# DeltaNet: the last inverse level as quarter-size products, and decay sums as two fp32r halves

## The chip, the cores and the metric

The kernel runs on one NeuronCore of a Trainium2 chip. The metric is device time in microseconds of one execution; the time before is 3436.42 us, the median of three runs (3434.37 to 3437.41). TensorE (PE) multiplies matrices, with its weight loads shown apart (PEld); VectorE (DVE), ScalarE (ACT) and GpSimd (POOL) work on tiles; SyncE (SP) issues most transfers.

## The reference, cut to what matters

The network has four layers, each a feed-forward block, a token mixer and a second feed-forward block. Layers 0 and 3 mix tokens with a bidirectional chunked gated DeltaNet of 8 heads of 128, on 128 context and 256 latent tokens; layer 1 is an attention layer, layer 2 a pooling mixer. The part that matters:

```
gcum = jnp.cumsum(cg(g), axis=-1)
diff = gcum[..., :, None] - gcum[..., None, :]
decay = jnp.where(incl, jnp.exp(jnp.where(incl, diff, 0.0)), 0.0)
lmat = jnp.where(strict, jnp.einsum('nbhid,nbhjd->nbhij', kb, k) * decay, 0.0)
amat = lmat + jnp.eye(CHUNK, dtype=F32)
sol = lax.linalg.triangular_solve(amat, rhs, left_side=True, lower=True, unit_diagonal=True)
attn = jnp.einsum('nbhid,nbhjd->nbhij', q, k) * decay
```

So there are exponentials of differences of running sums, and the solution of a unit triangular system for each chunk, head and direction. The kernel works on chunks of 128 tokens, which gives the same result.

## The kernel before, in words

Everything is written out by hand on each engine's queue; semaphores alone order the engines, and each queue runs in the order of the code.

A DeltaNet layer projects and convolves, then runs a *prelude*, a *decay stage* and three *waves*. There are 48 maps of 128 x 128 (3 chunks, 2 directions, 8 heads), handled four heads at a time in one PSUM bank of 512 columns, so twelve groups.

*Prelude* (`proj_a` on VectorE, start of `delta_net` on the others). TensorE forms the running sums; VectorE copies them to `dn_small` (L1425), forms their negative (`SM_NEG`, L1426) and the sum with the log of the gate (`SM_GB`, L1427) and signals `gcT_in`. TensorE, after the first two groups of key products, transposes the three 128 x 48 tables (L1968) and ScalarE copies them to `gcT` (L998), whose rows above 48 GpSimd has set to zero (L688).

*Decay stage.* For a group, `exponents` adds two things in a PSUM bank: a bf16 product that puts large negative numbers where the mask is off (L1953), and for each of four heads a product that spreads row `at` of `gcT` over all 128 partitions (L1957): the stationary operand is column `at` of the identity, broadcast to 128 columns. ScalarE takes the exponential with the other running sum as bias, four heads one by one (L1011), into a ring of three buffers (key half) or into `att` (query half). In the key half VectorE multiplies by the key products into `amap` (L1454), and GpSimd gathers the 16 x 16 diagonal blocks of the first eight groups (L702); for the last four VectorE copies them itself (L1452). The order is, six times: four key products, two decay groups; then six times: four query products, two decay groups, and ScalarE's copy of the query products (L1023). VectorE meanwhile inverts all diagonal blocks by forward substitution (L1466, L1467), transposes them (L1470, L1471) and spreads them into full tiles (L513), which needs the block mask that TensorE copies to PSUM after the whole stage (L1987). GpSimd spreads a second set (also L513).

*Waves.* A wave treats one chunk of each direction, in four groups `j`. It grows the inverse from blocks of 16 to 128 in three levels (4, 5, 6). For each level and group TensorE forms y = A'C (`y_product`, L2005), VectorE multiplies it with the level's mask into `W_Y` (L1500), TensorE forms z = B y (`z_product`, L2020) and VectorE subtracts it from the kept matrix (L1504). At levels 5 and 6 four transposes (`turn`, L2025) follow each y product, copied by ScalarE (L1040). At level 6, z updates C for the groups 0 and 1 and its transpose for 2 and 3. After it come the products with keys, values and state; value products of the first wave wait for GpSimd's `vb` (L726). After the last wave SP fetches the output weights, which lie in the same memory, once the last value products are done.

In the trace all products of four heads carry line L1932 (`four`). Each fp32 product of 128 x 128 is two TensorE instructions, so a group of four heads shows as x8; a transpose is one.

Of the kernel before, what the change touches and what calls it, by code (L numbers as in the profile page):

```python
# [46 lines left out]
LEVELS = (4, 5, 6)  # L47
WAVES = 3
# [83 lines left out]
def build(nc, inp, out, stages=3 * DEPTH):  # L132
# [143 lines left out]
    gcT = place("gcT", [P, 3, P], at=region_m + 11 * KB)  # L276
# [91 lines left out]
    gcT_zero, gcT_in, gcT_turned, gcT_copied = (sem(n) for n in ("gcT_zero", "gcT_in", "gcT_turned", "gcT_copied"))  # L368
# [259 lines left out]
    def _(pool):  # L628
# [50 lines left out]
        def delta_net(layer):  # L679
# [6 lines left out]
            pool.wait_ge(mask_in, 16 * (a + 1))  # L686
            pool.wait_ge(gc_done, a + 1)
            pool.memset(gcT[:], 0.0).then_inc(gcT_zero, 1)  # L688
# [108 lines left out]
    def _(act):  # L797
# [117 lines left out]
        def proj_a(ph):  # L915
# [81 lines left out]
            act.wait_ge(gcT_zero, a + 1)  # L997
            act.activation(gcT[0:MAPS], ps[5][0:MAPS, 0:T].rearrange("p (i c) -> p i c", i=3), ACT.Copy).then_inc(gcT_copied, 1)  # L998
# [188 lines left out]
    def _(dve):  # L1187
# [159 lines left out]
        def proj_a(ph):  # L1347
# [74 lines left out]
            steps.settle(dve.reciprocal(flat(SM_BETA), flat(SM_B)))  # L1422
            dve.wait_ge(gc_done, a + 1)
            both = dn_small[:, SM_GC:SM_TOTAL + 1].rearrange("p i c d h -> p (i c d h)")
            steps.settle(dve.tensor_copy(both, ps[4][:, 0:4 * NT * HEADS]))  # L1425
            dve.tensor_scalar(flat(SM_NEG), flat(SM_GC), -1.0, None, ALU.mult)  # L1426
            dve.tensor_tensor(flat(SM_GB), flat(SM_GC), flat(SM_NSP), ALU.add).then_inc(gcT_in, 1)  # L1427
# [3 lines left out]
        def delta_net(layer):  # L1431
# [3 lines left out]
            def bank(i):  # L1435
                return ps[i][:].rearrange("p (h c) -> p h c", h=GROUP)
# [56 lines left out]
            for w in range(WAVES):  # L1493
# [3 lines left out]
                for lev in LEVELS:  # L1497
                    for j in range(4):
                        mm(j, f"y{lev}")
                        dve.tensor_tensor(W_Y[j][:], bank(j), per_head(level_mask[lev - LEVELS[0]]), ALU.mult).then_inc(w_dve[j], 1)  # L1500
                    for j in range(4):
                        mm(j, f"z{lev}")
                        keep = (W_B if lev == LEVELS[-1] and j >= 2 else W_C)[w][j]
                        dve.tensor_tensor(keep, keep, bank(4 + j), ALU.subtract).then_inc(w_dve[j], 1)  # L1504
                    if w == 2 and lev == LEVELS[1]:
                        dve.wait_ge(c0_sq, a + 1)
                        dve.tensor_reduce(sumsq[:, 0:HEADS], first_sq, AX.X, ALU.add).then_inc(o_sum, 1)
# [228 lines left out]
    def _(pe):  # L1736
# [184 lines left out]
        def delta_net(layer):  # L1921
# [12 lines left out]

            def key_map(e):
                c, quad = MAP_ORDER[e]
                if e >= 2:
                    pe.wait_ge(amap_done, 2 * N_MAP * a + 2 * e - 2)
                keys = lambda h: k_of(c, GROUP * quad + h)
                four(e % 2, keys, keys).then_inc(kk_mm, 1)  # L1940
# [7 lines left out]
            def exponents(n, which, mask):  # L1948
# [6 lines left out]
                for h in range(GROUP):  # L1955
                    at = HEADS * (2 * c + d) + GROUP * quad + h
                    ins = pe.matmul(ps[bank][:, h * P:(h + 1) * P], ident[:, at:at + 1].to_broadcast([P, P]),  # L1957
                                    gcT[:, which], start=False, stop=h == GROUP - 1)
# [8 lines left out]
            for i, which in enumerate((SM_NEG, SM_GB, SM_GC)):  # L1967
                ins = pe.transpose(ps[5][0:MAPS, i * P:(i + 1) * P], dn_small[:, which].rearrange("p c d h -> p (c d h)"), ident[:])  # L1968
            ins.then_inc(gcT_turned, 1)
            pe.wait_ge(tok_v, HEADS * a + HEADS)  # L1970
# [18 lines left out]
            for w in range(WAVES):  # L1989
# [4 lines left out]
                def y_product(j, lev):  # L1994
# [10 lines left out]
                    four(j, lambda h: amap[:, i + h], lambda h: W_C[w][j][:, h]).then_inc(w_mm[j], 1)  # L2005

                def z_product(j, lev):
# [11 lines left out]
                    left, right = (W_Y[j], W_B[w][j]) if lev == LEVELS[-1] and j >= 2 else (W_B[w][j], W_Y[j])  # L2019
                    four(4 + j, lambda h: left[:, h], lambda h: right[:, h]).then_inc(w_mm[j], 1)  # L2020
# [334 lines left out]
```

## Time and profile before

| what | value |
|---|---|
| median of 3 runs | 3436.42 us |
| profiled execution | 3434.01 us, of it span 3432.2 us |
| mean granted TensorE clock | 0.984 of full |
| PE busy | 3296.7 us, 96% |
| DVE busy | 2521.7 us, 73% |
| ACT busy | 1370.7 us, 40% |
| POOL busy | 307.3 us, 9% |
| chain of waits | PE 89%, DVE 5%, POOL 2% |
| L1957 (decay sums) | x384 instructions, 50.6 us |

Times in the profile are of one execution. A busy matmul is counted from its start to its modelled end, so the instructions of a stream overlap: what one costs in a stream is the distance between starts, not its length. A row of the timeline merges equal neighbours (x8 is eight instructions), gives the start in us from the start of the span and the time from the first start to the last end, and in brackets how long the engine sat idle before and what released it. PEclk is the granted TensorE clock as a share of full (1.0 is 2.4 GHz, 0.5 is 1.2 GHz).

### The profile page before, as it was taken

Reading aid. Unit: us, or ns where it says so; the run is one execution under the profiler, and the core shown is the slowest. Engines: PE = TensorE matmul, PEld = TensorE weight load, DVE = VectorE, ACT = ScalarE, POOL = GpSimd, SP = SyncE. Lnnn points to the kernel's source line nnn. Section 1 sums busy time; section 2 is a strip of 40 time slices with the busy share of each in tenths; the row PEclk is TensorE's granted clock in tenths of the full one; section 3 lists DMA queues with packets and bytes.
Section 4 is the critical chain, followed back from the end, with each engine's and each line's share of the span. In section 5 each row is a group of like instructions: output and inputs, shape, how many; then the busy total and the mean of one; then the engine's idle time right before and its main releaser. Section 6 shows DMA issues by size and latency. Waiting matters only on the chain.

```text
span 3432.2 us, 50618 instructions
## 1 busy us (share of the span) xinstructions
PE 3296.7 (96%) x18244; PEld 3059.6 (89%) x18244; DVE 2521.7 (73%) x4167; ACT 1370.7 (40%) x2446; POOL 307.3 (9%) x360
## 2 busy tenths in 40 slices
PE   7999999989999999889999999999999999999998
PEld 7899898979998998868998998899899898998997
DVE  7888976667887885577887887788778886666444
ACT  2333556243334334354334333433433365534332
POOL 0000104520000001000000001000000000641001
PEclk9999999999999999999999999999999999999999
DMA  6555320034544553214553553355455431003331
GB/s 255 223 200 212 124 73 1 26 132 187 214 177 170 200 218 111 111 48 157 200 220 118 213 214 145 113 211 214 151 195 200 164 115 51 26 38 113 126 128 74
DMA packets 62772, 503.36 MB, mean 147 GB/s; under 512 B 6416, under 2 KB 14608, under 8 KB 16320
## 3 DMA queue, kind: packets, MB, share of 16 engines
q1 hardware_dynamic: 60512, 493.12, 37.4%
q0 software_dynamic: 2144, 8.68, 0.7%
q8 instruction: 74, 1.21, 0.1%
q14 instruction: 42, 0.34, 0.0%
HBM read 497.06 MB, written 4.72 MB: 146 GB/s over the span
## 4 chain that ended last, share of the span: by engine, by line
PE 89%; DVE 5%; POOL 2%; ACT 1%; issue 1%; DMA 1%; SPq 0%; DVEq 0%; POOLq 0%; ACTq 0%
PE bank L1742 77%; PE bank L1932 7%; PE bank L1957 1%; DMA mod_raw<-mod_w 1%; POOL x L658 1%; PE bank L2025 1%; PE bank L1883 1%; PE bank L1752 1%; POOL rstd L646 1%; DVE split_lo L1196 0%; DVE xS_lo L1266 0%; DVE mod_junk L427 0%; DVE xS_lo L1287 0%; DVE x L1345 0%; DVE xhat L1341 0%
## 5 line engine op out<-in xcount | busy, mean ns | idle before, releaser
L1742 PE MATMUL bank<-xS_hi,split_hi 128*128 128x386 f32 (+2 forms) x3344 | 1146.7, 343 | 22.5 <-DVE xS_lo L1266 13.4
L1742 PE MATMUL bank<-xS_lo,split_hi 128*128 128x386 f32 (+2 forms) x3344 | 1135.8, 340 | 0.0
L1742 PE MATMUL bank<-xS_hi,split_lo 128*128 128x386 f32 (+2 forms) x3344 | 1134.3, 339 | 0.0
L1196 DVE TENSOR_TENSOR split_lo<-raw,split_hi 128x1024 fp32r<-128x1024 f32 x644 | 779.0, 1217 | 285.6 <-ACT split_hi L810 285.5
L810 ACT ACTIVATE split_hi<-raw 128x1024 fp32r<-128x1024 f32 x644 | 653.2, 1053 | 486.0 <-DMA raw<-ffn_w 348.3
L427 DVE SCALAR_TENSOR_TENSOR mod_junk<-mod_raw,cond 128x1024 f32<-128x1024 f32 x536 | 655.6, 1223 | 61.5 <-DVE mod_junk L427 32.5
L1742 PEld LDWEIGHTS bank<-xS_hi,split_hi 128*128 128x128 f32 (+1 forms) x3344 | 628.9, 188 | 39.2 <-issue 15.3
L1742 PEld LDWEIGHTS bank<-xS_lo,split_hi 128*128 128x128 f32 (+1 forms) x3344 | 632.9, 189 | 10.2 <-issue 2.0
L1742 PEld LDWEIGHTS bank<-xS_hi,split_lo 128*128 128x128 f32 (+1 forms) x3344 | 630.7, 189 | 1.1
L1742 PE MATMUL bank<-split_hi,hid_hi 128*128 128x512 f32 x1056 | 415.7, 394 | 2.3 <-DVE hid_lo L1321 2.3
L1742 PE MATMUL bank<-split_hi,hid_lo 128*128 128x512 f32 x1056 | 413.9, 392 | 0.0
L1742 PE MATMUL bank<-split_lo,hid_hi 128*128 128x512 f32 x1056 | 411.0, 389 | 0.0
L900 ACT ACTIVATE silu_g<-gate_n 128x128 f32<-128x128 f32 x352 | 141.6, 449 | 585.6 <-DVE gate_n L1309 585.6
L658 POOL TENSOR_TENSOR x<-x,xhat 128x512 f32<-128x512 f32 x48 | 65.1, 1387 | 2137.2 <-DVE xhat L1341 2137.2
L1742 PEld LDWEIGHTS bank<-split_hi,hid_lo 128*128 128x128 f32 x1056 | 198.2, 188 | 45.9
L1742 PEld LDWEIGHTS bank<-split_hi,hid_hi 128*128 128x128 f32 x1056 | 198.1, 188 | 38.0 <-DVE hid_lo L1321 2.7
L905 ACT ACTIVATE hid_hi<-hidden 128x384 fp32r<-128x384 f32 x176 | 92.4, 525 | 349.1 <-DVE hidden L1317 349.1
L1742 PEld LDWEIGHTS bank<-split_lo,hid_hi 128*128 128x128 f32 x1056 | 198.4, 188 | 37.5
L1321 DVE TENSOR_TENSOR hid_lo<-hidden,hid_hi 128x384 fp32r<-128x384 f32 x176 | 98.2, 558 | 108.9 <-ACT hid_hi L905 108.9
L1313 DVE TENSOR_TENSOR up_n<-bank,rstd_bc 128x386 f32<-128x386 f32 x176 | 97.2, 553 | 76.3 <-PE bank L1742 76.3
L1742 PE MATMUL bank<-split_hi,xS_hi 128*128 128x384 f32 (+2 forms) x360 | 134.9, 375 | 16.3 <-DVE xS_lo L1575 7.8
L1360 DVE SCALAR_TENSOR_TENSOR scratch<-scratch,cols 128x193 f32<-128x193 f32 x384 | 131.1, 415 | 13.1 <-ACT scratch L934 13.1
(262 smaller groups left out, 3279.6 us busy)
## 6 DMA issues: line engine op xcount, KB each, us to landing
raw<-ffn_w SPq DMA_DIRECT2D x176, 1536.0 KB, 7.6
mod_raw<-mod_w SPq DMA_DIRECT2D x134, 1024.0 KB, 4.8
raw<-a_in_w SPq DMA_DIRECT2D x20, 1536.0 KB, 6.3
raw<-b_in_w SPq DMA_DIRECT2D x8, 1536.0 KB, 6.4
raw<-a_out_w SPq DMA_DIRECT2D x4, 1536.0 KB, 7.7
mod_first<-mod_w SPq DMA_DIRECT2D x5, 1024.0 KB, 21.5
mod_first<-mod_rows SPq DMA_DIRECT2D x5, 1024.0 KB, 23.5
raw<-b_out_w SPq DMA_DIRECT2D x2, 1536.0 KB, 6.2
```

Of the source, the lines that this page charges most:

```text
L427: eng.scalar_tensor_tensor(mod_junk[:], weights[:, t], 1.0, cond[:, c], ALU.mult, ALU.mult, accum_out=mod_column(layer, unit, t, c)).then_ ...
L646: pool.tensor_tensor(rstd[:, span], rstd[:, span], neg_half[:, span], ALU.pow).then_inc(ready, 1)
L658: pool.tensor_tensor(x[:, t, span], x[:, t, span], xhat[:, t, span], ALU.add).then_inc(res_pool, 1)
L810: act.activation(split_hi[:, unit.slot, q, 0:w], raw[:, unit.slot, q, 0:w], ACT.Copy).then_inc(hi_ready, 1)
L900: ins = act.activation(silu_g[:, par, lo:hi], gate_n[:, par, lo:hi], ACT.Silu, bias=gate_n[:, par, T + c:T + c + 1])
L905: act.activation(hid_hi[:, par], hidden[:, par], ACT.Copy).then_inc(hid_hi_done, 1)
L1196: dve.tensor_tensor(split_lo[:, unit.slot, q, 0:w], raw[:, unit.slot, q, 0:w], f32(split_hi[:, unit.slot, q, 0:w]), ALU.subtract).then_inc ...
L1313: dve.tensor_tensor(up_n[:, par], ps[BANK_UP][:, 0:TC], rstd_bc[:], ALU.mult).then_inc(up_norm, 1)
L1321: dve.tensor_tensor(hid_lo[:, par], hidden[:, par], f32(hid_hi[:, par]), ALU.subtract).then_inc(hid_done, 1)
L1360: dve.scalar_tensor_tensor(dst, src, weight, dst, ALU.mult, ALU.add).then_inc(conv_step, 1)
L1742: ins = pe.matmul(out, lhsT, rhs, start=start and i == 0, stop=stop and i == 2)
L1932: ins = pe.matmul(ps[bank][:, h * P:(h + 1) * P], lhsT(h), rhs(h), start=True, stop=True)
```

## The change

Two things change in the DeltaNet layers.

First, the decay sums. Each of the three tables is split by VectorE into a high half, rounded to fp32r, and the rest, both fp32r, side by side in `halves` (columns 0 to 47 and 64 to 111; GpSimd clears the tile). The transposed table has the high halves in rows 0 to 47 and the rests in rows 64 to 111, on 128 partitions, as fp32r. The stationary operand of the spreading product is a column of `two_hot`, with ones in rows `at` and `at` + 64, so one fp32r product sums both halves.

Second, level 6. The matrices are triangular in blocks of 64, so only one 64 x 64 quarter of y and of z is not zero. `quarter` forms just this one per head, from 64 x 64 operands; VectorE copies that quarter of y without a mask and subtracts that quarter of z.

```diff
-    gcT = place("gcT", [P, 3, P], at=region_m + 11 * KB)
+    gcT = place("gcT", [P, 3, P], F32R, at=region_m + 11 * KB)
+    halves = place("halves", [P, 3, 2, 64], F32R, at=region_m + 13 * KB)
+    two_hot = place("two_hot", [P, MAPS], F32R, at=region_m + 10 * KB + 768)
...
+            pool.memset(f32(halves[:]), 0.0).then_inc(halves_zero, 1)
             pool.wait_ge(gc_done, a + 1)
-            pool.memset(gcT[:], 0.0).then_inc(gcT_zero, 1)
...
-            act.wait_ge(gcT_zero, a + 1)
-            act.activation(gcT[0:MAPS], ps[5][0:MAPS, 0:T].rearrange("p (i c) -> p i c", i=3), ACT.Copy).then_inc(gcT_copied, 1)
+            act.activation(gcT[:], ps[5][:, 0:T].rearrange("p (i c) -> p i c", i=3), ACT.Copy).then_inc(gcT_copied, 1)
...
+            dve.wait_ge(halves_zero, a + 1)
+            dve.tensor_tensor(two_hot[:], ident[:, 0:MAPS], ident[:, 64:64 + MAPS], ALU.add).then_inc(two_hot_ready, 1)
             dve.wait_ge(gc_done, a + 1)
...
-            dve.tensor_scalar(flat(SM_NEG), flat(SM_GC), -1.0, None, ALU.mult)
-            dve.tensor_tensor(flat(SM_GB), flat(SM_GC), flat(SM_NSP), ALU.add).then_inc(gcT_in, 1)
+            steps.settle(dve.tensor_scalar(flat(SM_NEG), flat(SM_GC), -1.0, None, ALU.mult))
+            steps.settle(dve.tensor_tensor(flat(SM_GB), flat(SM_GC), flat(SM_NSP), ALU.add))
+            for i, which in enumerate((SM_NEG, SM_GB, SM_GC)):
+                dve.tensor_copy(halves[:, i, 0, 0:MAPS], flat(which)).then_inc(halves_hi, 1)
+            for i, which in enumerate((SM_NEG, SM_GB, SM_GC)):
+                dve.wait_ge(halves_hi, 3 * a + i + 1)
+                ins = dve.tensor_tensor(halves[:, i, 1, 0:MAPS], flat(which), f32(halves[:, i, 0, 0:MAPS]), ALU.subtract)
+            ins.then_inc(gcT_in, 1)
...
-                        dve.tensor_tensor(W_Y[j][:], bank(j), per_head(level_mask[lev - LEVELS[0]]), ALU.mult).then_inc(w_dve[j], 1)
+                        if lev == LEVELS[-1]:
+                            ins = dve.tensor_copy(W_Y[j][FIRST, :, SECOND], bank(j)[FIRST, :, SECOND])
+                        else:
+                            ins = dve.tensor_tensor(W_Y[j][:], bank(j), per_head(level_mask[lev - LEVELS[0]]), ALU.mult)
+                        ins.then_inc(w_dve[j], 1)
...
-                        keep = (W_B if lev == LEVELS[-1] and j >= 2 else W_C)[w][j]
-                        dve.tensor_tensor(keep, keep, bank(4 + j), ALU.subtract).then_inc(w_dve[j], 1)
+                        keep, of = W_C[w][j], bank(4 + j)
+                        if lev == LEVELS[-1]:
+                            keep, of = (W_B[w][j][SECOND, :, FIRST], of[SECOND, :, FIRST]) if j >= 2 else (keep[FIRST, :, SECOND], of[FIRST, :, SECOND])
+                        dve.tensor_tensor(keep, keep, of, ALU.subtract).then_inc(w_dve[j], 1)
...
+            def quarter(bank, rows_of, cols_of, lhsT, rhs):
+                for h in range(GROUP):
+                    out_of = ps[bank][rows_of, h * P + cols_of.start:h * P + cols_of.stop]
+                    ins = pe.matmul(out_of, lhsT(h), rhs(h), start=True, stop=True)
+                return ins
...
-                    ins = pe.matmul(ps[bank][:, h * P:(h + 1) * P], ident[:, at:at + 1].to_broadcast([P, P]),
+                    ins = pe.matmul(ps[bank][:, h * P:(h + 1) * P], two_hot[:, at:at + 1].to_broadcast([P, P]),
                                     gcT[:, which], start=False, stop=h == GROUP - 1)
...
-            for i, which in enumerate((SM_NEG, SM_GB, SM_GC)):
-                ins = pe.transpose(ps[5][0:MAPS, i * P:(i + 1) * P], dn_small[:, which].rearrange("p c d h -> p (c d h)"), ident[:])
+            for i in range(3):
+                ins = pe.transpose(ps[5][:, i * P:(i + 1) * P], f32(halves[:, i]).rearrange("p o c -> p (o c)"), ident[:])
...
-                    four(j, lambda h: amap[:, i + h], lambda h: W_C[w][j][:, h]).then_inc(w_mm[j], 1)
+                    if lev == LEVELS[-1]:
+                        quarter(j, FIRST, SECOND, lambda h: amap[SECOND, i + h, FIRST], lambda h: W_C[w][j][SECOND, h, SECOND]).then_inc(w_mm[j], 1)
+                    else:
+                        four(j, lambda h: amap[:, i + h], lambda h: W_C[w][j][:, h]).then_inc(w_mm[j], 1)
...
-                    left, right = (W_Y[j], W_B[w][j]) if lev == LEVELS[-1] and j >= 2 else (W_B[w][j], W_Y[j])
-                    four(4 + j, lambda h: left[:, h], lambda h: right[:, h]).then_inc(w_mm[j], 1)
+                    if lev < LEVELS[-1]:
+                        ins = four(4 + j, lambda h: W_B[w][j][:, h], lambda h: W_Y[j][:, h])
+                    elif j < 2:
+                        ins = quarter(4 + j, FIRST, SECOND, lambda h: W_B[w][j][FIRST, h, FIRST], lambda h: W_Y[j][FIRST, h, SECOND])
+                    else:
+                        ins = quarter(4 + j, SECOND, FIRST, lambda h: W_Y[j][FIRST, h, SECOND], lambda h: W_B[w][j][FIRST, h, FIRST])
+                    ins.then_inc(w_mm[j], 1)
```

On VectorE, at the end of the prelude of layer 0, the order before, where L1425 is the copy of the running sums and L1427 the step that the transposes wait for:

```order
L1422 RECIPROCAL dn_small<-dn_small 128x48
L1425 COPY dn_small<-bank 128x96
L1426 TENSOR_SCALAR dn_small<-dn_small 128x48
L1427 TENSOR_TENSOR dn_small<-dn_small 128x48
L1428 TENSOR_TENSOR dn_small<-dn_small 128x48
```

The same place in the changed kernel (its lines are numbered higher; L1437 is now the step that the transposes wait for):

```order
L1425 RECIPROCAL dn_small<-dn_small 128x48
L1427 TENSOR_TENSOR two_hot<-ident 128x48
L1430 COPY dn_small<-bank 128x96
L1431 TENSOR_SCALAR dn_small<-dn_small 128x48
L1432 TENSOR_TENSOR dn_small<-dn_small 128x48
L1434 CAST halves<-dn_small 128x48 x3
L1437 TENSOR_TENSOR halves<-dn_small,halves 128x48 x3
L1439 TENSOR_TENSOR dn_small<-dn_small 128x48
```

The new stationary operand stands before the copy, the six steps of the split between the running sums and the transposes.

On TensorE, level 6 of the first wave before (`wk_116` to `wk_119` are C of the four groups, `wk_120` to `wk_123` B, `wk_124` to `wk_127` the y; `ident` marks a turn), from the last y product on and with the first value product behind it:

```order
L1932 MATMUL bank<-wk_119,amap 128x128 x4
L2025 MATMUL bank<-ident,wk_119 128x128 x4
L1932 MATMUL bank<-wk_124,wk_120 128x128 x4
L1932 MATMUL bank<-wk_125,wk_121 128x128 x4
L1932 MATMUL bank<-wk_122,wk_126 128x128 x4
L1932 MATMUL bank<-wk_123,wk_127 128x128 x4
L1932 MATMUL bank<-wk_124,wk_116 128x128 x4
```

The same in the changed kernel, where the names are higher by two:

```order
L1955 MATMUL bank<-wk_121,amap 64x64 x4
L2057 MATMUL bank<-ident,wk_121 128x128 x4
L1955 MATMUL bank<-wk_126,wk_122 64x64 x4
L1955 MATMUL bank<-wk_127,wk_123 64x64 x4
L1955 MATMUL bank<-wk_124,wk_128 64x64 x4
L1955 MATMUL bank<-wk_125,wk_129 64x64 x4
L1949 MATMUL bank<-wk_126,wk_118 128x128 x4
```

Nothing changes place there: the y and z products are quarters, and the full-size turns stand between them as before.

## Rows read from the trace of the kernel before

**Rows 1.** The page's first line.

```profile
span 3432.2 us, 50618 instructions
```

**Rows 2.** Chain of waits in layer 0: start, us, what, count.

```profile
540.92 0.89 PE bank L1957 x8
...
634.53 29.70 PE bank L1932 x264
```

**Rows 3.** Timeline of TensorE, decay stage: start, us, engine, line, operation, shapes, count.

```profile
539.43 0.38 PE L1953 MATMUL bank<-dn_const 128*128 128x512 bf16 x1
...
539.65 1.05 PE L1957 MATMUL bank<-gcT,ident 128*128 128x128 f32 x8
```

**Rows 4.** Timeline of ScalarE, decay stage, idle before and releaser in brackets.

```profile
535.47 4.46 ACT L1011 ACTIVATE wk<-bank,dn_small 128x128 f32<-128x128 f32 x16 [1.07 <-PE bank L1957]
...
543.90 2.25 ACT L1011 ACTIVATE wk<-bank,dn_small 128x128 f32<-128x128 f32 x8 [0.86 <-PE bank L1957]
...
565.59 2.25 ACT L1011 ACTIVATE att<-bank,dn_small 128x128 f32<-128x128 f32 x8 [0.38 <-PE bank L1957]
```

**Rows 5.** Timeline of VectorE and GpSimd, decay stage and its end.

```profile
537.55 15.07 POOL L702 COPY blocks<-amap 32x128 f32<-32x128 f32 x32 [4.50 <-DVE amap L1454]
...
548.25 1.53 DVE L1452 TENSOR_TENSOR blocks<-bank,wk 32x128 f32<-32x128 f32 x4 [1.38 <-ACT wk L1011]
...
574.09 6.17 POOL L513 TENSOR_TENSOR wk<-bc,dn_const 128x512 f32<-128x512 f32 x4 [21.48 <-DVE bc L1471]
...
575.40 4.25 DVE L513 TENSOR_TENSOR wk<-cc,bank 128x512 f32<-128x512 f32 x4 [1.46 <-PE bank L1987]
```

**Rows 6.** Timeline of the prelude, VectorE and TensorE.

```profile
531.80 0.20 DVE L1427 TENSOR_TENSOR dn_small<-dn_small 128x48 f32<-128x48 f32 x1
...
533.00 0.49 PE L1968 MATMUL bank<-ident,dn_small 128*48 128x128 f32 x3
```

**Rows 7.** Timeline of TensorE, level 6 of the second wave.

```profile
629.04 1.06 PE L1932 MATMUL bank<-amap 128*128 128x128 f32 x8
...
629.94 0.60 PE L2025 MATMUL bank<-ident,amap 128*128 128x128 f32 x4
...
634.36 3.74 PE L1932 MATMUL bank<-wk,wk 128*128 128x128 f32 x32
```

**Rows 8.** Timeline of GpSimd, end of the first wave.

```profile
599.63 4.03 POOL L726 TENSOR_TENSOR wk<-dn_v,dn_small 128x512 f32<-128x512 f32 x4 [4.58 <-PE bank L1932]
```

**Rows 9.** Groups by line and form (us, mean ns), and one timeline row.

```profile
L1932 PEld LDWEIGHTS bank<-wk,wk 128*128 128x128 f32 x576 | 65.9, 192 | 0.0
...
L1742 PEld LDWEIGHTS bank<-xS_hi,split_hi 128*32 128x32 f32 x16 | 1.7, 109 | 1.2
...
529.65 1.40 PE L1903 MATMUL bank<-dn_small,tri 128*128 128x8 f32 x12
```

**Rows 10.** Timeline of TensorE, square sums and the attention layer.

```profile
516.59 1.45 PE L1883 MATMUL bank<-scratch,ones 128*128 128x384 f32 x4
...
1470.15 0.92 PE L2155 MATMUL bank<-kT,qT 64*128 64x384 f32 x4
...
1472.15 0.92 PE L2155 MATMUL bank<-kT,qT 64*128 64x384 f32 x4
```

**Rows 11.** Stretches (us, busy by engine, clock), and TensorE's first y products.

```profile
1452.00:1456.00 4.00, 2.78 (x18) 1.82 (x19) 2.99 (x13) 3.16 (x18) 0.00 (x0) 0.96 0.00 0
1456.00:1462.00 6.00, 6.00 (x26) 4.15 (x27) 4.65 (x20) 3.89 (x20) 0.00 (x0) 0.50 0.00 0
1470.00:1496.00 26.00, 23.95 (x144) 14.64 (x143) 23.91 (x56) 19.07 (x57) 1.87 (x2) 1.00 0.00 1
2960.00:2966.00 6.00, 6.00 (x39) 5.89 (x39) 5.35 (x7) 2.14 (x1) 6.00 (x6) 0.72 0.00 0
...
576.49 4.38 PE L1932 MATMUL bank<-wk,amap 128*128 128x128 f32 x32 [1.19 <-DVE wk L513]
...
2959.78 5.65 PE L1932 MATMUL bank<-wk,amap 128*128 128x128 f32 x32 [1.19 <-DVE wk L513]
```

More of the change, by code:

```diff
@@ L47 @@
 LEVELS = (4, 5, 6)
+FIRST, SECOND = slice(0, P // 2), slice(P // 2, P)
 WAVES = 3
@@ L366, in build @@
     state_in, state_stored = sem("state_in"), sem("state_stored")
-    gcT_zero, gcT_in, gcT_turned, gcT_copied = (sem(n) for n in ("gcT_zero", "gcT_in", "gcT_turned", "gcT_copied"))
+    gcT_in, gcT_turned, gcT_copied = (sem(n) for n in ("gcT_in", "gcT_turned", "gcT_copied"))
+    halves_zero, halves_hi, two_hot_ready = (sem(n) for n in ("halves_zero", "halves_hi", "two_hot_ready"))
     kk_mm, kq_mm, kq_copied, att_done = sem("kk_mm"), sem("kq_mm"), sem("kq_copied"), sem("att_done")
@@ L1966, in delta_net @@
             pe.wait_ge(gcT_in, a + 1)
-            for i, which in enumerate((SM_NEG, SM_GB, SM_GC)):
-                ins = pe.transpose(ps[5][0:MAPS, i * P:(i + 1) * P], dn_small[:, which].rearrange("p c d h -> p (c d h)"), ident[:])
+            for i in range(3):
+                ins = pe.transpose(ps[5][:, i * P:(i + 1) * P], f32(halves[:, i]).rearrange("p o c -> p (o c)"), ident[:])
             ins.then_inc(gcT_turned, 1)
+            pe.wait_ge(two_hot_ready, a + 1)
             pe.wait_ge(tok_v, HEADS * a + HEADS)
```

## The prediction

> **What bounds the kernel now.** I read the page first, for the span and the two places where the changed lines run: two DeltaNet layers (about 531 to 700 us and 2912 to 3083 us) in a span that is otherwise feed-forward and projection work, which the diff leaves alone [rows 1]. Then the chain of waits inside layer 0: it sits on TensorE nearly throughout, first on the decay sums (L1957), later on 29.70 us of uninterrupted four-head products in one stretch [rows 2]. So an instruction saved on TensorE is worth its issue time, as long as nobody else becomes last. The timelines then say who would be last, stage by stage.
>
> *Decay stage.* A decay group is one bf16 mask product and four fp32 products. The mask takes 0.22 us (539.43 to 539.65), the four fp32 products are eight instructions [rows 3]; their last leaves at the pace of 0.89 us per eight seen in the chain [rows 2], 0.112 us each. One round is four key products (0.89) and two such groups: 0.89 + 2 x (0.22 + 0.89) = 3.11 us. ScalarE confirms it: 2.25 us of exponentials, then 0.86 us idle until PE [rows 4]; in the query half it also copies the query products and idles 0.38 us per round. So TensorE paces both halves, six rounds each. At the end VectorE waits: its substitution chain is done by 574.0 (POOL starts then on `bc`), but its L513 idles 1.46 us more, until TensorE has passed the query half and copied the mask [rows 5].
>
> *Level 6 of a wave.* Four times a y product (629.04 to 629.94, 0.90 us) and a turn of four transposes, together 5.32 us until 634.36, so 1.33 each and 0.43 for the turn; then four z products, 32 instructions at 0.112 us, 3.58 us [rows 7]; TensorE never stops, VectorE and ScalarE wait for it. There are six waves, three in each layer.
>
> **The change, part by part.**
>
> *Decay sums as fp32r.* Each fp32 product becomes one instruction instead of two, so a group falls from 0.22 + 8 x 0.112 to 0.22 + 4 x 0.112 = 0.67 us and a round to 0.89 + 1.33 = 2.23. No row shows an fp32r product with only 128 moving columns. Its bounds: no gain at all (0.89 for the four, as now), and 0.055 each, half of what I take. I take 0.112, because every product here that loads 128 stationary columns comes no faster than that, even with 8 moving columns: 12 in 1.40 us [rows 9]. The low end would not help: sixteen exponentials run in 4.46 us when nothing holds them, 0.273 us each [rows 4], so ScalarE needs 2.18 us per round and is last at either price. It then also starts 0.45 us earlier, since the first group is shorter.
>
> What that moves: VectorE starts the ninth map at 548.25 [rows 5]. With ScalarE running through, nine maps are ready at 535.47 - 0.45 + 9 x 1.09 = 544.9, 3.3 us earlier. From there VectorE's chain (block copies, substitution, transposes) is its own work and keeps its length. GpSimd's gathers run 15.07 us from the first map, one after another; they would end at 552.2 and VectorE asks for them at about 553.5: hidden, with 1.3 us to spare. TensorE's and ScalarE's chain gains more, 6 x (3.11 - 2.2) + 6 x 0.38 = about 7 us, so the 1.46 us wait goes too. Per layer: 3.3 + 1.46 = 4.75 us.
>
> *The prelude that pays for it.* VectorE adds the stationary operand with two ones before it waits for the sums (hidden), and after them two settled steps, three casts and three subtractions of 48 columns. A step of 48 columns lasts 0.20 us, and the last that the transposes need ends at 532.0 now [rows 6]. Two steps are now waited out and six come behind them, partly overlapping: an estimate of 0.9 us, so 532.9. TensorE does not start the transposes before 533.00, because the first key products stand ahead [rows 6]; they become wider, 128 stationary columns for 48. I charge 0.15 us, bounds 0 and 1 us (the whole delay uncovered). Behind the waiting transposes stand all decay groups, so this shifts the layer. Net 4.6 us per layer, 9.2 us in all.
>
> *Level 6 as quarters.* Of each 128 x 128 product a 64 x 64 one remains: still eight instructions per group of four heads, with half the stationary and half the moving columns. No row shows one. By columns it is 8 x 0.056 = 0.45 us; by instruction count it stays 0.89. The nearest row is the weight load of 32 columns, 109 ns against 192 for 128 [rows 9]: 83 ns less for 96 columns, so 55 less for 64, which halves the 112 ns spacing. I take 0.45: 8 groups x 0.44 = 3.55 us saved per wave, bounds 0 and 3.55.
>
> *What the quarters add.* They use half the rows of the array and alternate with full transposes. A row on such alternation is in the attention layer: four instructions with 64 rows, then three transposes and six full products, all in 2.00 us (1470.15 to 1472.15) [rows 10]. At 0.32 us per 384 columns of fp32 (four in 1.45 us with the tail of the last) two halves side by side would take 0.64, the nine others 9 x 0.112 = 1.01; 0.35 us is left over for a change in and a change out. So a change costs between 0 and 0.17 us; I take 0.10, between the ends. A wave has ten (into and out of each y, into and out of the z block): 1.0 us. The Trainium skill, page "TensorEngine Tiling (Array Packing)", section Key Properties, says that changing the tiling mode drains the TensorE; it gives no price. This trace agrees that something is left over, 0.35 us per pair.
>
> *GpSimd becomes last once.* In the first wave the value products wait for `vb`, four GpSimd steps in 4.03 us that start after the first z product [rows 8]. TensorE used to need 3.6 us for the z products; with 1.8 us it catches up, and the fourth value product starts about 0.37 us late: 0.74 us for two layers. In the other waves the next work needs only the state, and VectorE's halved eviction keeps up (256 columns a step for 512). VectorE's 48 shortened steps are worth nothing by themselves, since TensorE is what they wait for.
>
> Level 6: 6 x (3.55 - 1.0) - 0.74 = 14.6 us.
>
> *Clock.* TensorE idles about 3 us between the mask copy and the first y product after the change, where it idled 1.2 us. In layer 3 the first y products already run slow: 5.65 us for 32 instructions against 4.38 in layer 0, with a granted clock of 0.72 over that stretch, so part of it at the lower of the two levels (1.2 GHz) [rows 11]. I assume layer 0 now pays those 1.3 us too (bounds 0 and 1.3).
>
> **The sum.** 9.2 + 14.6 - 1.3 = 22.5 us off. The profiled execution took 3434.01 us around its span, the median of the runs is 3436.42; the loss in between is outside these stages, so I take 22.5 from the median: 3413.9, say 3414 us. After the waves everything hangs on their end (the output weights are fetched after the last value products), so the gain is kept.
>
> **The rivals.**
> 1. *fp32r at 128 columns is no faster than fp32.* For it: the narrowest use in this kernel is wider. Against it: half the instructions. Then the decay part gives -0.3 and no 1.3 us of clock: 14.6 - 0.3 = 14.3 off, 3422 us.
> 2. *The clock falls at level 6.* For it: after 4 us of the attention layer with TensorE 2.78 us busy, on 64-row products among others, the granted clock was 0.50, the lower level, for the next 6 us. Against it: busy for 23.95 of 26 us with the same mixture it kept 1.00 [rows 11]. One fall costs 1.3 us; one in each wave 7.8 us: 3422 us. Two in each: 3430.
> 3. *Quarters go by instruction count.* For it: the instruction count is unchanged. Then level 6 gives only the ten changes: -6.0, and the sum is 9.2 - 1.3 - 6.0 = 1.9 off: 3434.5 us, no change.
> 4. *The other side: the drain.* If each of the 60 changes waits for the array to empty and for the next load, the price decides from (9.2 - 1.3 + 6 x 3.55 - 0.74) / 60 = 0.47 us on; at 0.6 us the sum is 36 - 28.5 = 7.5 us slower, 3444 us. For it: the leftover of the attention row. Against it: the same row caps it at 0.17.
>
> **How the numbers follow.** Forecast with changes at 0 to 0.17 us: 3407 to 3419, chance 0.60. Rival 1: 0.18, rival 2: 0.12, rival 3: 0.06, rival 4: 0.04. The range 3406 to 3427 holds the forecast, rival 1 and most of rival 2. A measurement of this kernel tells a change from none at about 0.2%, 6.9 us. Faster than 3429.5: the forecast, rival 1 and most of rival 2, 0.89; within: rival 3 and the rest, 0.07; slower: 0.04.
>
> **What would show it.** Right: ScalarE's exponentials without a gap in the key half, decay groups 0.67 us apart at most, VectorE's ninth map 3 us earlier after the first exponential, L513 no longer released by TensorE, y groups of level 6 at 0.45 to 0.6 us and z blocks below 2 us. Wrong: four fp32r products in 0.89 us; gaps of over 0.2 us on TensorE at every switch between a quarter and a transpose; a granted clock under 1.0 within the waves; a wait of VectorE's turn for GpSimd's gathers.

## The result, and the profile after

| | median | runs | lowest to highest |
|---|---|---|---|
| before | 3436.79 us | 4 | 3434.37 to 3437.41 |
| changed | 3415.86 us | 4 | 3414.66 to 3417.19 |

The ratio is 0.9943, 95% interval 0.9931 to 0.9955: 20.9 us faster, inside the forecast range and 1.9 us from the forecast. In a second set of runs the changed kernel took 3417.58 us (5 runs) against 3435.40 of the kernel before (9 runs): 0.9947, interval 0.9934 to 0.9961, 17.8 us.

The profiled execution of the changed kernel took 3416.66 us; its first page line answers to [rows 1]:

```profile
span 3414.9 us, 50246 instructions
```

The two spans differ by 17.3 us. Because a few stretches at a lower granted clock come and go from one execution to the next, I compare the two DeltaNet layers by offsets. In each I take the start of VectorE's copy of the running sums (L1425 before, L1430 after) as zero and read where five events start:

| start, us after the copy of the sums | before, layer 0 | before, layer 3 | after, layer 0 | after, layer 3 |
|---|---|---|---|---|
| VectorE's block copy of the ninth map | 16.84 | 18.49 | 15.16 | 15.17 |
| VectorE's spreading (L513, now L517) | 43.99 | 45.63 | 40.90 | 40.90 |
| from first y to first z product | 4.22 | 5.49 | 6.61 | 5.24 |
| products with keys, first wave | 74.23 | 77.13 | 71.93 | 70.57 |
| work after the last wave | 169.45 | 172.36 | 162.94 | 161.58 |

Layer 0 gives 6.51 us and layer 3 gives 10.78, together 17.29: the whole difference of the spans lies here. But 2.9 us of it (172.36 - 169.45) are stretches that layer 3 of the kernel before ran at a lower clock in this one profile; a second profile of it, further down, has none in either layer. From the key products on (two waves) both layers go from 95.2 to 91.01 us.

*Decay groups.* Timeline of TensorE, changed kernel, in the key half, whose six rounds are four key products and two decay groups each (start, us, engine, line, operation, shapes, count; in brackets idle time before and releaser). L1976 is the mask product, L1980 the decay products, L1949 the key products:

```profile
534.16 0.38 PE L1976 MATMUL bank<-dn_const 128*128 128x512 bf16 x1 [0.78 <-ACT gcT L1001]
534.18 0.74 PE L1980 MATMUL bank<-gcT,two_hot 128*128 128x128 f32 x4
534.77 0.39 PE L1976 MATMUL bank<-dn_const 128*128 128x512 bf16 x1
...
537.98 1.16 PE L1949 MATMUL bank<-qkvz 128*128 128x128 f32 x8 [1.18 <-DVE amap L1465]
...
542.80 1.16 PE L1949 MATMUL bank<-qkvz 128*128 128x128 f32 x8 [0.25 <-DVE amap L1465]
```

Groups start 0.61 us apart (534.16, 534.77), where [rows 3] stood for 1.11: one fp32r product takes half the time of an fp32 one. But the key products of the third round (those of the first two stand ahead of all decay groups) wait 1.18 us for VectorE, a wait that the forecast did not have; those of the fifth wait 0.25 us. ScalarE's timeline shows what that does:

```profile
535.02 4.25 ACT L1014 ACTIVATE wk<-bank,dn_small 128x128 f32<-128x128 f32 x16 [0.73 <-PE bank L1980]
539.85 4.36 ACT L1014 ACTIVATE wk<-bank,dn_small 128x128 f32<-128x128 f32 x16 [0.58 <-PE bank L1980]
544.67 3.33 ACT L1014 ACTIVATE wk<-bank,dn_small 128x128 f32<-128x128 f32 x12 [0.46 <-PE bank L1980]
```

Sixteen exponentials, those of two rounds, run through; then TensorE is late by 0.58 us and, two rounds on, by 0.46. That is less than the 0.86 us in every round of [rows 4], but not the stream without a gap that was forecast.

*Prelude.* VectorE's timeline (first three rows) and GpSimd's (last) at the sums:

```profile
530.75 0.26 DVE L1430 COPY dn_small<-bank 128x96 f32<-128x96 f32 x1 [1.49 <-PE bank L1921]
531.04 0.73 DVE L1431 TENSOR_SCALAR dn_small<-dn_small 128x48 f32<-128x48 f32 x1
531.80 0.21 DVE L1432 TENSOR_TENSOR dn_small<-dn_small 128x48 f32<-128x48 f32 x1
...
530.77 0.96 POOL L693 MEMSET bb<- 128x1024 f32 x1 [146.93 <-PE bank L1921]
```

The negation L1431 takes 0.73 us beside GpSimd's clearing of `bb`, which started just before it and ends at 531.73. Before, the same 48-column step (L1426) took 0.19 us; there the clearing of `gcT` stood ahead of that of `bb`, which came only behind it:

```profile
531.70 0.19 DVE L1426 TENSOR_SCALAR dn_small<-dn_small 128x48 f32<-128x48 f32 x1
...
531.79 0.99 POOL L689 MEMSET bb<- 128x1024 f32 x1
```

From the copy of the sums to the first decay group it is now 3.41 us (530.75 to 534.16), where it was 2.70 (531.41 to 534.11).

*End of the decay stage.* VectorE and GpSimd, answering to [rows 5]:

```profile
545.91 1.55 DVE L1463 TENSOR_TENSOR blocks<-bank,wk 32x128 f32<-32x128 f32 x4 [0.98 <-ACT wk L1014]
...
571.65 4.01 DVE L517 TENSOR_TENSOR wk<-cc,bank 128x512 f32<-128x512 f32 x4
...
537.11 15.19 POOL L706 COPY blocks<-amap 32x128 f32<-32x128 f32 x32 [5.12 <-DVE amap L1465]
```

L517 has no wait in brackets any more. GpSimd's gathers end at 552.30, and VectorE asks for them at 554.56: hidden.

TensorE there, and the table by stretches (length, then busy us and count of PE, PEld, DVE, ACT and POOL, then granted clock, DMA share and GB/s):

```profile
564.74 4.51 PE L1935 MATMUL bank<-ident,qkvz 128*128 128x128 f32 x24 [4.28 <-ACT att L1014]
...
572.85 6.77 PE L1949 MATMUL bank<-wk,amap 128*128 128x128 f32 x32 [2.48 <-DVE wk L517]
```

```profile
564.00:573.00 9.00, 5.15 (x27) 4.72 (x27) 8.52 (x19) 7.60 (x13) 1.24 (x1) 0.77 0.00 0
573.00:580.00 7.00, 7.00 (x37) 7.00 (x38) 4.98 (x7) 0.90 (x1) 7.00 (x6) 0.57 0.01 2
592.00:599.00 7.00, 6.95 (x83) 5.89 (x83) 3.70 (x9) 2.39 (x4) 2.04 (x3) 1.00 0.00 0
```

TensorE is done early and idles 4.28 us; the 24 transposes behind that take 4.51 us and the first y products 6.77 for the 32 instructions that took 4.38 in [rows 11], at a granted clock of 0.57, so mostly at the lower of its two levels (1.2 GHz). At level 6 (592 to 599) it is back at 1.00.

*Level 6.* TensorE in the first wave; L1955 are quarters, L2057 turns:

```profile
592.01 0.68 PE L1955 MATMUL bank<-wk,amap 64*64 64x64 f32 x8
592.62 0.66 PE L2057 MATMUL bank<-ident,wk 128*128 128x128 f32 x4
593.21 0.68 PE L1955 MATMUL bank<-wk,amap 64*64 64x64 f32 x8
...
596.78 1.90 PE L1955 MATMUL bank<-wk,wk 64*64 64x64 f32 x32
598.72 4.12 PE L1949 MATMUL bank<-wk,wk 128*128 128x128 f32 x32
```

A y group costs 0.61 us, a turn now 0.59 (0.43 before), the z block 1.94 instead of 3.58. The whole level takes 6.71 us (592.01 to 598.72), where [rows 7] give 8.90 for the second wave. The weight loads show the change from a turn to a quarter as idle time that is nobody's wait:

```profile
592.62 0.42 PEld L2057 LDWEIGHTS bank<-ident,wk 128*128 128x128 f32 x4
593.21 0.54 PEld L1955 LDWEIGHTS bank<-wk,amap 64*64 64x64 f32 x8 [0.17 <-issue]
```

*GpSimd's `vb`* takes what it took in [rows 8], and the 32 value products stretch from 3.74 to 4.12 us (row 598.72 above):

```profile
597.54 4.04 POOL L730 TENSOR_TENSOR wk<-dn_v,dn_small 128x512 f32<-128x512 f32 x4 [4.96 <-PE bank L1955]
```

### The profile page after: what moved, and what is told of

It reads as the page before. It is cut to its first block, busy times and chain, and to the rows that moved or that the text cites. A ratio compares the mean times of both kernels' runs of the same rounds, so it can differ in the third digit from the quotient of the medians.

```text
span 3414.9 us, 50246 instructions
## 1 busy us (share of the span) xinstructions
PE 3268.5 (96%) x18052; PEld 3026.2 (89%) x18052; DVE 2511.8 (74%) x4181; ACT 1369.7 (40%) x2446; POOL 307.8 (9%) x360
## 3 DMA queue, kind: packets, MB, share of 16 engines
q8 instruction: 72, 1.18, 0.1%
## 4 chain that ended last, share of the span: by engine, by line
PE 87%; DVE 7%; POOL 2%; ACT 1%; issue 1%; DMA 1%; SPq 0%; DVEq 0%; POOLq 0%; ACTq 0%
PE bank L1759 77%; PE bank L1949 5%; DMA mod_raw<-mod_w 1%; POOL x L662 1%; PE bank L1955 1%; PE bank L2057 1%; PE bank L1900 1%; DVE mod_junk L431 1%; DVE xS_lo L1269 1%; POOL rstd L650 1%; DVE split_lo L1199 0%; DVE x L1348 0%; PE bank L1769 0%; DVE xhat L1344 0%; DVE xS_lo L1290 0%
```

## The experiments

**Each part alone.** The first kernel is the changed one with level 6 as it was (full products, VectorE's masked product and full subtraction); the diff shows TensorE's part. The second is the kernel before with the quarters only, the same lines the other way round:

```diff
-                    if lev == LEVELS[-1]:
-                        quarter(j, FIRST, SECOND, lambda h: amap[SECOND, i + h, FIRST], lambda h: W_C[w][j][SECOND, h, SECOND]).then_inc(w_mm[j], 1)
-                    else:
-                        four(j, lambda h: amap[:, i + h], lambda h: W_C[w][j][:, h]).then_inc(w_mm[j], 1)
+                    four(j, lambda h: amap[:, i + h], lambda h: W_C[w][j][:, h]).then_inc(w_mm[j], 1)
...
+                    left, right = (W_Y[j], W_B[w][j]) if lev == LEVELS[-1] and j >= 2 else (W_B[w][j], W_Y[j])
+                    four(4 + j, lambda h: left[:, h], lambda h: right[:, h]).then_inc(w_mm[j], 1)
```

> The change's decay sums alone; level 6 in full-size products as in the kernel before. Theory A (the stage gained 3.1 us per layer in the trace of the changed kernel, not the 4.6 forecast, and lost part of it again in slow first y products): 3 to 6 us under the kernel before, about 3432. Theory B (the forecast's sizes hold, 9.2 less 1.3): 7.9 us under, 3429. If both parts only add up to the whole change when the clock is counted with each: this run and the level-6 run together give 17 to 24 us.

> The change's quarter products of level 6 alone; decay sums in fp32 as before. Theory A (a wave's level 6 takes 6.7 us instead of 8.9, 2.2 us less, six times, less 0.4 us per layer for GpSimd): 12.4 us under the kernel before, about 3424, and the first y products of layer 0 run as in the kernel before, 4.4 us for 32 instructions, since TensorE has no long idle time ahead of them. Theory B (forecast, 0.10 us per change between quarter and full products): 14.6 us under, 3422.

Decay alone: 3428.07 us (11 runs) against 3435.22 (15 runs), ratio 0.9980 (0.9971 to 0.9989), 7.2 us off, more than the 3 to 6 expected. Level 6 alone: 3420.20 us (5 runs), ratio 0.9958 (0.9945 to 0.9972), 15.0 us off. Their sum, 22.2, lies in the expected 17 to 24, 1.3 us above the 20.9 of the first set for both together and 4.4 above the 17.8 of the second. In the trace of level 6 alone both layers read +16.85, +43.99, 4.18, +72.49 and +163.50 in the terms of the table: the work after the last wave comes 5.95 us earlier than in layer 0 before, 11.9 us for both layers. The spans of the two profiles differ by 15.0 us too (3432.2 against 3417.2), and there the other 3 us are what layer 3 of the kernel before lost to its clock (172.36 - 169.45). That the median's 15.0 holds the same 3 us is not shown. In the trace of decay alone the work after the last wave stands at +168.56 and +167.51, in layer 0 with a fall of the clock in the prelude.

**Fewer changes of size.** The changed kernel, but at level 6 the four turns stand behind the four y products, so a wave has 4 changes between quarter and full size instead of 10:

```diff
                     for j in range(4):
                         y_product(j, lev)
-                        if lev > LEVELS[0]:
+                        if lev == LEVELS[1]:
                             turn(j)
+                    for j in range(4 if lev == LEVELS[-1] else 0):
+                        turn(j)
```

> The changed kernel with the four turns of level 6 behind its four y products instead of between them: four changes between quarter and full products per wave instead of ten, nothing else. Theory A (each change costs 0.13 to 0.16 us of TensorE): level 6 of a wave falls from 6.7 to about 5.8 us, 5 us less than the changed kernel in six waves, about 3411. Rival (the time lies in each small product and in the transposes themselves, not in the change): no difference, 3416. Second rival (z products then wait for ScalarE's copies of the turns): gaps ahead of the z products, 3414 to 3418.

It took 3410.13 us (5 runs), ratio 0.9929 (0.9915 to 0.9942), 5.7 us under the first median of the changed kernel. TensorE at level 6:

```profile
593.18 2.07 PE L1955 MATMUL bank<-wk,amap 64*64 64x64 f32 x32
595.19 1.97 PE L2057 MATMUL bank<-ident,wk 128*128 128x128 f32 x16
597.09 1.90 PE L1955 MATMUL bank<-wk,wk 64*64 64x64 f32 x32
599.03 4.12 PE L1949 MATMUL bank<-wk,wk 128*128 128x128 f32 x32
```

5.85 us for the level instead of 6.71. Over two waves (from the key products to the end) 89.28 instead of 91.01 us, so 0.87 us per wave for six changes: 0.144 us each. The same work in another order, with no wait of TensorE inside the level in either trace, so this is the price of a change itself. Both rivals fall: the time is not in the small products, and no gap stands ahead of the z products (597.09).

**TensorE kept busy.** The changed kernel with 18 more mask products into an unused bank after the last decay group, and 10 after the mask copy; nobody reads them:

```diff
+            pe.wait_ge(amap_done, 2 * N_MAP * (a + 1))
+            keep_busy(18)
             pe.wait_ge(decay_exp, N_DECAY * (a + 1))
...
             pe.matmul(ps[7][:, 0:P], ident[:], block_mask, start=True, stop=True).then_inc(mask_copied, 1)
+            keep_busy(10)
```

> The changed kernel with TensorE kept busy where it idles ahead of the first y products: 18 mask products of 512 columns into a free bank before the wait for the last exponentials, 10 after the copy of the block mask; their result is used by nobody. Theory A (the idle time of over 4 us there is what lowers the granted clock, and the slow first y products cost 2.4 us in layer 0): turns of the keys back from 4.5 to 2.8 us, first y products back from 6.8 to about 4.4 us per 32, 2 to 5 us under the changed kernel, about 3412. Rival (VectorE's spreading of the inverse paces the first y products whatever the clock): y products stay at 4.4 to 5 us but the end moves by less than 1 us.

3413.73 us (5 runs), ratio 0.9937 (0.9923 to 0.9951), 2.1 us under the first median of the changed kernel. TensorE ahead of the y products in layer 0, and the clock there:

```profile
564.89 2.84 PE L1935 MATMUL bank<-ident,qkvz 128*128 128x128 f32 x24 [0.37 <-ACT att L1014]
...
573.01 4.08 PE L1949 MATMUL bank<-wk,amap 128*128 128x128 f32 x32 [1.67 <-DVE wk L517]
```

```profile
573.00:580.00 7.00, 6.99 (x60) 6.96 (x61) 6.75 (x10) 0.00 (x0) 7.00 (x6) 1.00 0.00 0
```

Work that nobody needs brings the transposes back to 2.84 us and the y products to 4.08. From the first y to the first z product it is 3.92 and 3.89 us in the two layers. The work after the last wave stands at +160.26 in layer 0, 2.7 us earlier than in the changed kernel, so VectorE's spreading did not set the pace there and the rival falls.

**Four banks for the key products; the clearing later; all four edits.** Three more kernels ran beside the changed kernel on one chip. In the first, VectorE reads the key products from the same four banks, and the first two groups of query products, which use banks 6 and 7, now wait until those are free; the diff shows TensorE's part for the keys. In the second GpSimd waits for `gcT_in`, the signal behind VectorE's split. The third has both, the turns behind and the fillers.

```diff
+KEY_BANK = (0, 1, 6, 7, 0, 1)
...
-                if e >= 2:
-                    pe.wait_ge(amap_done, 2 * N_MAP * a + 2 * e - 2)
+                if e >= 4:
+                    pe.wait_ge(amap_done, 2 * N_MAP * a + 2 * e - 6)
...
-                four(e % 2, keys, keys).then_inc(kk_mm, 1)
+                four(KEY_BANK[e], keys, keys).then_inc(kk_mm, 1)
```

```diff
+            pool.wait_ge(gcT_in, a + 1)
             steps.settle(pool.memset(bb[:], 0.0))
```

> The changed kernel itself once more, on the chip on which the three kernels below run: 3415 to 3418 us, if the 3415.86 us of its first runs holds. The three below are to be read against this time.

> The changed kernel with the key products spread over four PSUM banks (0, 1, 6, 7) instead of two, so that key products of a round no longer wait for VectorE's products of two rounds earlier. Theory (the bank is what kept the key half from being gapless): ScalarE's idle 0.58 and 0.46 us in the key half go, the ninth map starts at +14.1 instead of +15.16 us after the copy of the sums, VectorE's L517 at +39.9 instead of +40.90, and the time falls by 2 us in two layers. Rival (the ring of three buffers, which VectorE frees, holds ScalarE just as long): the gaps stay under another name, ninth map at +15.1, no change. Second rival (GpSimd's gathers become last): ninth map earlier, L517 not.

> The changed kernel with GpSimd's clearing of its 16 x 16 blocks (0.96 us) moved behind the signal that the sums are ready, so that it no longer runs beside VectorE's negation of the sums (L1431). Theory (the two engines hold each other up on SBUF): L1431 takes 0.19 us instead of 0.73, the first decay group starts at +2.9 instead of +3.41 us after the copy of the sums, 0.5 us a layer, 1.1 us in all. Rival (the negation is slow for what stands before it on its own engine): it stays at 0.73 us, no change.

> The changed kernel with all four edits: turns of level 6 behind its four y products, TensorE kept busy with 18 and 10 further mask products around the mask copy (into an unused bank, their result is not read), four banks for the key products, and the later clearing. If the four gains are independent, 5.7 + 2.1 + 2.0 + 1.1 = 10.9 us under the changed kernel, 3405 us. Rival (gains in the key half only lengthen the wait that follows, because VectorE's chain or the clock absorbs them): 5.7 + 2.1 alone, 3408 us.

| kernel (5 runs each) | median, us | ratio to before, 95% interval |
|---|---|---|
| changed, again | 3417.58 | 0.9947, 0.9934 to 0.9961 |
| four banks | 3413.98 | 0.9937, 0.9923 to 0.9950 |
| later clearing | 3414.63 | 0.9941, 0.9928 to 0.9955 |
| all four edits | 3404.22 | 0.9909, 0.9895 to 0.9922 |

Four banks, ScalarE and VectorE in layer 0:

```profile
536.06 11.45 ACT L1015 ACTIVATE wk<-bank,dn_small 128x128 f32<-128x128 f32 x44 [0.73 <-PE bank L1983]
...
545.55 1.55 DVE L1464 TENSOR_TENSOR blocks<-bank,wk 32x128 f32<-32x128 f32 x4 [0.41 <-ACT wk L1015]
```

ScalarE runs 44 of its 48 exponentials without a gap, and the ninth map stands at +13.76 instead of +15.16, L518 at +39.52 instead of +40.90: 1.4 us in layer 0, more than the 1.0 expected. The rival with the ring of three buffers falls up to the ninth map; the ring holds ScalarE once, for 0.33 us ahead of the last four. Later clearing, VectorE and GpSimd:

```profile
531.55 0.19 DVE L1432 TENSOR_SCALAR dn_small<-dn_small 128x48 f32<-128x48 f32 x1
...
532.87 0.95 POOL L694 MEMSET bb<- 128x1024 f32 x1 [148.49 <-DVE halves L1438]
```

The negation takes 0.19 us again, and the ninth map stands at +14.67 and +14.67: 0.49 us a layer. The medians of the two fell by 3.6 and 3.0 us, more than the 2.8 and 1.0 that two layers give by these offsets; the rest is not accounted for. With all four edits the ninth map stands at +13.28 in both layers. The kernel is 13.4 us under the changed one, 2.5 more than the sum of the expected gains, and 31.2 us under the kernel before. Its fillers did not always help: from the first y to the first z product it is 3.91 us in layer 3, but 5.40 in layer 0, where TensorE still idles 1.74 us ahead of the y products.

**Where the clock falls.** The kernel before profiled again, and all four edits with 16 instead of 10 fillers behind the mask copy:

```diff
-            keep_busy(10)
+            keep_busy(16)
```

> The kernel before, profiled once more, for the places where TensorE's granted clock falls. Theory (a fall belongs to where TensorE idled just before, so it is fixed by the order of the work): layer 3 again starts its ninth map at +18.5 us after the copy of the sums and takes 5.5 us from the first y product to the first z product, layer 0 +16.84 and 4.2. Rival (a fall hits any of several weak places by the moment at which it comes): the same losses of 1.1 to 1.6 us stand elsewhere, or only once.

> The kernel with all four edits once more, beside the next one: 3402.7 to 3405.9 us as before.

> The kernel with all four edits, with 16 instead of 10 mask products behind the mask copy, which leaves TensorE about 0.3 us of idle time instead of 1.74 us ahead of the first y products. Theory (what TensorE does just ahead of the y products decides their clock): layer 0 takes 3.9 us from the first y to the first z product instead of 5.40, 1.5 us in all. Rival (the fall comes from somewhere else, so filling this gap does nothing): no change, 3404 us. Cost if the fillers run over: up to 1 us slower.

In the second profile of the kernel before (one run, 3432.48 us) both layers read +16.85, +44.00, 4.17 to 4.18 and +169.42: no fall at these places, so the theory of a fixed place is wrong and the rival stays. TensorE in layer 3:

```profile
2953.41 2.84 PE L1918 MATMUL bank<-ident,qkvz 128*128 128x128 f32 x24 [1.24 <-ACT att L1011]
...
2958.90 4.34 PE L1932 MATMUL bank<-wk,amap 128*128 128x128 f32 x32 [1.20 <-DVE wk L513]
```

All four edits took 3404.39 us (4 runs), with more fillers 3403.40 (4 runs, ratio 0.9901, 0.9884 to 0.9917). From y to z it is 3.91 and 3.90 us in the two layers, but 3.89 and 3.92 with 10 fillers in this run too: the 5.40 us did not come back, so whether the six more are worth anything is not settled.

Taken over all 13 profiles, the 24 transposes ahead of the y products and the time from the first y to the first z product sort by what TensorE did before:

| TensorE ahead of the transposes | DeltaNet layers | transposes, us | first y to first z, us |
|---|---|---|---|
| fp32 decay groups, idle 1.2 us | 6 | 2.84 | 4.2 in five, 5.49 in one |
| fp32r decay groups, idle 4.2 to 4.3 us | 12 | 4.28 to 5.38 | 5.2 to 6.6 in eleven, 3.94 in one |
| fp32r decay groups and fillers, idle 0.4 us | 8 | 2.84 | 3.9 in seven, 5.40 in one |

So the slow transposes come with the long idle time every time, and the slow y products nearly so; the one at 3.94 (later clearing, layer 3) had 4.22 us of idle time ahead like the others.

## Why the prediction was right, point by point

The time came out near the forecast, but the terms of the sum did not. The decay stage gave 6.2 us, not 9.2; level 6 gave 11.9, not 14.6; and the first y products lost 3.4 us in the two layers of the first profile, not 1.3. By the traces that makes 14.7 us instead of 22.5, and directly the two layers of the changed kernel are 14.3 us shorter than those of the second profile of the kernel before (2 x 169.42 against 162.94 + 161.58). The medians moved by 20.9 us in the first set and by 17.8 in the second. So that the number fell so close to the forecast is partly luck.

Without falls of the clock a DeltaNet layer takes 169.42 us before (second profile) and 160.26 after (kept busy, layer 0), 9.2 us less; 0.3 of that is the y products with the fillers ahead (3.9 us instead of 4.2).

*fp32r at 128 columns: right.* Expected 0.112 us each; from the second to the fourth product of a group they start 0.11 us apart. The group is 0.61 us and not 0.67, since the second product starts 0.27 to 0.29 us after the mask product, where 0.22 and one product of 0.112 were expected. Rival 1 falls.

*"ScalarE needs 2.18 us per round and is last at either price": the step that failed.* The forecast put the ninth map 3.3 us earlier, less 0.15 for the prelude; it came 1.68 earlier. TensorE's key products write one of two banks, and the bank comes free only when VectorE has used its last round. Before, TensorE was late anyhow and never met that wait; with shorter decay groups it does, and 1.4 us go there (four banks). So ScalarE was last only as long as TensorE had no wait of its own. The prelude was charged 0.15 us; the six steps of the split and the slowed negation delay the first decay group by 0.71 us, of which 0.49 are the clearing (later clearing). The first decay group is 0.5 us shorter, so the first exponential starts 0.21 us late. With both obstacles away the ninth map comes 3.56 us earlier, a little over the forecast: the chain behind it was read right, and the 1.46 us wait of L513 went as forecast. (The "about 7 us" of TensorE's and ScalarE's chain is 7.7 by its own terms; nothing hung on it.) Decay: 3.1 us a layer instead of 4.6, 6.2 instead of 9.2.

*Why the negation was slow.* Row: 0.73 us, ended 0.04 us after GpSimd's memset; 0.19 with the memset elsewhere. The Trainium skill, page "SBUF — State Buffer", section "SBUF: two separate sides", says that VectorE, in some of its modes, and GpSimd share a pair of ports that whoever starts first holds for its whole instruction, while the other blocks. The trace agrees: memset first, and the negation ends when it has ended. It is not every step of VectorE that is held: before, L1427, which adds two operands, took 0.20 us [rows 6] inside the clearing of `bb` (531.79 to 532.78).

*Level 6: right in kind, the change mis-sized.* By the measured 0.144 us ten changes cost 1.44 us per wave, not 1.0, though within the bounds of 0 and 0.17 each; a wave gained 2.11 us (95.22 to 91.01 over two), and 2.11 + 1.44 = 3.55 is the gross saving forecast. With GpSimd's 0.38 us per layer, which the value products show (4.12 against 3.74), it is 11.9 us instead of 14.6. A change costs a third of the 0.47 us that rival 4 needed, and from a turn to a quarter it shows as 0.17 us of idle weight load; the rule on draining in the Trainium skill, page "TensorEngine Tiling (Array Packing)", section Key Properties, agrees with that row, and the price comes from the runs. Rivals 3 and 4 fall, the third because eight quarter instructions take about 0.5 us.

*Clock.* Rival 2 falls: the granted clock is 1.00 at level 6 (592 to 599), and over the waves from 52 to 150 us after the copy of the sums in all 26 layers of the 13 profiles. The term for the first y products had the right place and was too small. TensorE now idles 4.2 to 4.3 us ahead of the transposes where it idled 1.24, and the first y products lost 1.0 to 2.4 us in every layer of the two profiles (5.24 to 6.61 against 4.2). The kernel before lost 1.3 there in one of four layers. The forecast took the slow y products of layer 3 before for a fixed cost; the second profile shows that they were chance. What helped the forecast is that the kernel before lost time to its clock as well: 2.9 us in layer 3 of the first profile, none in the second, whose 3432.48 us lie 4 us under the median of seven runs beside it. In the 32 runs of the kernel before from the later sets, the eight with a mean granted clock of 0.984 or 0.985 took 3432.5 to 3434.1 us and the 24 at 0.982 or 0.983 took 3434.4 to 3438.7. That suggests, without showing where, that most runs behind its median lost time to the clock. How much of the 20.9 us is that, no run here separates.

*Left open.* In 7 of 26 layers profiled (13 profiles) the stretch up to the ninth map took 1.0 to 1.7 us longer than in the other layer or profile of the same kernel, as layer 3 of the kernel before did in the table; before and after the change and in either layer. In all seven the granted clock was 0.72 from 1 us before the copy of the sums to 5 us after it; in the other 19 layers it was 1.00. Which execution meets it, the runs don't tell.

## What to carry to other kernels

When one engine's group gets shorter, look for the buffer that it fills two rounds ahead: a wait that was always met becomes the next limit, and two more banks gave 1.4 us a layer. Group products of one tile size together: 36 changes fewer gave 5.2 us in the trace. And look at what TensorE does in a gap that an improvement opens: filling it with products that nobody reads took the first y products from 5.24 and 6.61 us to 3.9, in seven of the eight layers that had them. Last, compare the parts and not only the total: here two terms too large and time that the kernel before lost made a sum that looked right.

## What the runs showed of the hardware

- A change between 64 x 64 and 128 x 128 products costs TensorE 0.144 us, in either direction about the same. In the trace of the changed kernel the first quarter instruction starts 0.20 us after a turn's last transpose and the second 0.11 us after the first, where 0.11 and 0.06 pass without a change. The first transpose starts 0.15 us after the last quarter instruction and the second 0.165 us after the first, where 0.06 and 0.11 pass without a change.
- An fp32r product of 128 x 128 by 128 columns comes every 0.11 us, an fp32 one of two instructions every 0.22; a 64 x 64 fp32 quarter by 64 columns, also two instructions, every 0.12.
- A one-input VectorE step of 48 columns (L1431) beside a GpSimd memset took 0.73 us instead of 0.19; a two-input one (L1427 before) beside a memset took 0.20.
- Behind 4.2 to 4.3 us of idle time TensorE's 24 transposes took 4.28 to 5.38 us instead of 2.84 in all 12 layers that had it; in the changed kernel the granted clock was 0.77 from 564 to 573 us.
